# Two layers of a hybrid-heads and mixture-of-experts backbone: differential maps joined ahead of the turn, token lists in two stages, broadcast vectors issued later

## The reference

```python
def layer(x, xc, l):                      # 256 latent and 256 context tokens
    h = rmsnorm(x, norm1_g) * (1 + mod[1]) + mod[0]          # mod = silu(c) @ w_ada + b_ada
    y_a = window_attention(4 heads, with sinks)
    # differential attention, 4 heads of two maps each
    p = softmax(q0 @ k0.T) - lam * softmax(q1 @ k1.T);  y_b = rmsnorm(p @ v) * (1 - lam_init)
    y_c = latent_attention(4 heads);  y_d = gated_delta_net(4 heads, both directions)
    x = x + mod[2] * (concat(y_a, y_b, y_c, y_d) @ w_out)
    h = rmsnorm(x, norm2_g) * (1 + mod[4]) + mod[3]
    idx, w = top 6 of 64 experts for each token              # 4 of 8 groups first
    f = sum over idx of w * (silu(h @ w_gate[e]) * (h @ w_up[e])) @ w_down[e]
    x = x + mod[5] * (f + shared(h))                         # context alike in layer 0; layer 1 is latent only
```

## Time and profile before

| | |
|---|---|
| time, median of 3 executions | 2381.39 us (2380.7 to 2386.14) |
| time of the profiled execution | 2381.21 us |
| span of the profiled execution | 2379.4 us |
| PE busy | 2027.9 us, 85% |
| DVE busy | 705.3 us, 30% |
| ACT busy | 482.3 us, 20% |
| POOL busy | 261.7 us, 11% |
| moved by DMA | 558.55 MB, mean 235 GB/s |
| PE clock granted, mean share | 0.921 |

### The profile page before, as it was taken

The page is one execution under the profiler, slowest core; times in us unless marked ns, Lnnn a source line. Parts: engine busy times, 40 slices in busy tenths (PEclk is TensorE's granted clock), DMA queues, the critical chain, the costliest instruction groups (busy, mean ns, idle before and its releaser), DMA issues.

```text
span 2379.4 us, 33780 instructions
## 1 busy us (share of the span) xinstructions
PE 2027.9 (85%) x13844; PEld 1157.5 (49%) x13844; DVE 705.3 (30%) x1540; ACT 482.3 (20%) x1106; POOL 261.7 (11%) x312
## 2 busy tenths in 40 slices
PE   4999899979789999999993598899878888888982
PEld 2455578974534444444441356689753333333331
DVE  1121266651551111111113531666261111111114
ACT  1111265430201111111110211544211111111111
POOL 3000001210101111111110000022010111111110
PEclk9999999989789999999996699999888999999996
DMA  9576400001089999999987210100139999999963
GB/s 318 204 265 235 152 12 2 4 7 53 36 326 386 421 407 400 389 375 372 386 341 288 93 35 27 45 2 4 59 155 385 395 390 418 402 404 406 393 267 128
DMA packets 136120, 558.55 MB, mean 235 GB/s; under 512 B 27424, under 2 KB 60925, under 8 KB 85917
## 3 DMA queue, kind: packets, MB, share of 16 engines
q1 hardware_dynamic: 109757, 494.74, 52.0%
q0 software_dynamic: 24192, 38.54, 4.7%
q10 hardware_dynamic: 2016, 23.07, 2.3%
HBM read 556.26 MB, written 46.14 MB: 253 GB/s over the span
## 4 chain that ended last, share of the span: by engine, by line
PE 62%; DMA 23%; DVE 8%; ACT 2%; SPq 2%; issue 2%; POOL 0%; POOLq 0%; DVEq 0%; ACTq 0%
PE bank L760 55%; DMA arena<-in_moe_w_up 14%; DMA ring<-in_moe_w_up 7%; PE bank L763 6%; DVE arena L1268 2%; DVE arena L1265 1%; DMA arena<-y_rows 1%; DMA ring<-in_w_ada 1%; SPq L567 1%; ACT h_t L1909 1%; ACT arena L1909 1%; SPq L496 1%; DVE x_t L1268 1%; DVE arena L1291 1%; DVE arena L1809 1%
## 5 line engine op out<-in xcount | busy, mean ns | idle before, releaser
L760 PE MATMUL bank<-ring,arena 128*64 128x512 f32 (+4 forms) x2688 | 722.7, 523 | 70.1 <-DMA ring<-in_moe_w_up 47.1
L760 PE MATMUL bank<-arena 64*64 64x64 f32 (+6 forms) x5836 | 711.5, 323 | 44.9 <-DMA arena<-in_moe_w_up 21.0
L760 PEld LDWEIGHTS bank<-arena 64*64 64x64 f32 (+4 forms) x5836 | 367.8, 148 | 237.5 <-issue 222.6
L760 PEld LDWEIGHTS bank<-ring,arena 128*64 128x64 f32 (+3 forms) x2688 | 270.9, 152 | 367.1 <-issue 354.2
L763 PE MATMUL bank<-cst,arena 128*128 128x128 f32 (+2 forms) x1462 | 228.8, 296 | 124.6 <-DVE arena L1268 100.2
L1906 ACT ACTIVATE arena<-bank 128x256 f32<-128x256 f32 (+5 forms) x472 | 212.0, 459 | 587.7 <-PE bank L760 379.8
L763 PEld LDWEIGHTS bank<-cst,arena 128*128 128x128 f32 (+2 forms) x1462 | 190.1, 175 | 269.7 <-issue 131.5
L1265 DVE TENSOR_TENSOR arena<-arena,bank 128x256 f32<-128x256 f32 (+2 forms) x112 | 47.6, 425 | 740.5 <-ACT arena L1909 720.2
L760 PE MATMUL bank<-ring,h_t 128*128 128x384 f32 (+5 forms) x800 | 211.9, 427 | 17.4 <-ACT h_t L1909 17.4
L2308 POOL DMA_INDIRECT y_rows<-h_t,arena x80 | 80.4, 1005 | 933.7 <-DVE h_t L1844 933.7
L1909 ACT ACTIVATE arena<-bank 128x256 f32<-128x256 f32 (+1 forms) x86 | 33.4, 388 | 734.6 <-PE bank L760 734.6
(11 more groups left out here) (169 smaller groups left out, 1159.0 us busy)
## 6 DMA issues: line engine op xcount, KB each, us to landing
ring<-in_moe_w_gate SPq DMA_DIRECT2D x78, 1024.0 KB
ring<-in_moe_w_up SPq DMA_DIRECT2D x78, 1024.0 KB
ring<-in_moe_w_down SPq DMA_DIRECT2D x78, 1024.0 KB, 18.1
arena<-in_moe_w_gate SPq DMA_DIRECT2D x50, 1024.0 KB
arena<-in_moe_w_up SPq DMA_DIRECT2D x50, 1024.0 KB
arena<-in_moe_w_down SPq DMA_DIRECT2D x50, 1024.0 KB, 18.0
ring<-in_w_ada SPq DMA_DIRECT2D x52, 576.0 KB, 5.2
arena<-y_rows ACTq DMA_DIRECT2D x6, 3072.0 KB, 12.8
```

Of the source, the lines that this page charges most:

```text
L760: return pe.matmul(o, a, b, start=first, stop=last)
```

## The change

It has three parts.

1. **Differential maps** (`turned`, `turn_no`). When both exponentials of a differential head are there, DVE takes the reciprocals of their two sums, multiplies the second with the negative `lam` and the first map's sum, and adds the second map, so weighted, to the first. Only this one map is turned, copied and multiplied with the values. Turning comes one step later (two behind the scores) and the value product three behind, for all maps. `PX` has eight buffers in place of four; the added four lie in a slot of the ring. The scaling at the tile's end covers half the width.
2. **Token lists in two stages.** DVE makes 8 of the 16 rounds, which is enough for the pairs; three pairs lead the order of units. The other 8 rounds stand behind the copies of gathered rows of units 0 and 1, four each, and the whole units' lists are ordered on PE behind `up` of unit 1. The shared expert's products and sums are placed differently among them, and `down_bank` changes.
3. **Start.** POOL zeroes the padding, waits for PE's step `mod.turn 2` (the last before the projections) and then issues the 35 small transfers.

```diff
-    units, i = [(r,) for r in range(FIXED)], 0
-    for j, pair in enumerate(pairs):
-        upto = len(whole) * (j + 1) // n
+    units, i = [(r,) for r in range(FIXED)] + pairs[:RING], 0
+    for j, pair in enumerate(pairs[RING:]):
+        upto = len(whole) * (j + 1) // (n - RING)
...
-            return 2 + m % 6
+            return (4, 5, 2, 3, 6, 7, 1, 4)[m]
...
+        def turned(step):
+            return (2 * step, 2 * step + 1) if step % 8 < 4 else (2 * step,)
+        def turn_no(u):
+            return 12 * (u // 16) + (u % 16 if u % 16 < 8 else 4 + u % 16 // 2)
...
-                    for u in (2 * step - 2, 2 * step - 1):
+                    for u in turned(step - 2):
                         if 0 <= u < 2 * pairs:
-                            wait('ACT', 'att.exp', l, u)
+                            if u % 16 < 8:
+                                wait('ACT', 'att.exp', l, u)
+                            else:
+                                wait('DVE', 'att.less', l, u)
...
-                    for u in (2 * step - 4, 2 * step - 3):
+                    for u in turned(step - 3):
...
-                wait('DVE', 'rt.list', l, CAP // 8 - 1)
+                wait('DVE', 'rt.list', l, HALF // 8 - 1)
...
-                mm(bank[1][:, 0:full], LST[:, 0:CAP], PERM[:, 0:full])
...
+                    if u == 1:
+                        wait('DVE', 'rt.list', l, CAP // 8 - 1)
+                        mm(bank[7][:, 0:full], LST[:, 0:CAP], PERM[:, 0:full]).then_inc(*done('PE', 'rt.rest', l))
...
+                    u = 2 * step - 2
+                    if 0 <= u < 2 * pairs and u % 16 >= 8:
+                        wait('ACT', 'att.exp', l, u + 1)
+                        dve.reciprocal(RINV[:, i, m:m + 2], SUMS[:, i, m:m + 2]).then_inc(*done('DVE', 'att.rinv', l, i, m))
+                        wait('DVE', 'att.rinv', l, i, m)
+                        stt(RINV[:, i, m + 1:m + 2], RINV[:, i, m + 1:m + 2], lamt[:, 4:5], SUMS[:, i, m:m + 1]).then_inc(*done('DVE', 'att.share', l, u))
+                        wait('DVE', 'att.share', l, u)
+                        stt(PX[u % 8][:, 0:n], PX[(u + 1) % 8][:, 0:n], RINV[:, i, m + 1:m + 2], PX[u % 8][:, 0:n], ALU.mult, ALU.add
+                            ).then_inc(*done('DVE', 'att.less', l, u))
...
-                for r in range(CAP // 8):
-                    if r in (2, 7):
-                        shared_act((2, 7).index(r))
+                for r in range(HALF // 8):
+                    list_round(r)
+                    if r == 4:
+                        shared_act(1)
+                    if r == 6:
+                        shared_add(0)
...
+                    if isinstance(e, int) and e < 2:
+                        for n in range(4):
+                            list_round(HALF // 8 + 4 * e + n)
...
+            pool.memset(GP, 0.0).then_inc(*done('Pool', 'pad.zero', 0))
+            wait('PE', 'mod.turn', 0, 2)
             load_vectors(0)
             load_rows(pool, 1)
             load_vectors(1)
...
+                        if u == 0:
+                            wait('DVE', 'rt.tok2', l)
                         gather_rows(u + RING)
```

More of the change, by code:

```diff
@@ L266, in build @@
         CV, _ = area(at, 6, T)
-        CQT0, _ = area(at, 512)
-        PX = [PX3[:, q] for q in range(3)] + [area(at + 512, 512)[0]]
+        PX = [PX3[:, q] for q in range(3)] + [area(at + 512, 512)[0]] + [ring[:, 2 * SLOT + 2048 + 512 * q:2 * SLOT + 2560 + 512 * q] for q in range(4)]
         CQT, at = area(at, 2, T, parts=96)
@@ L950, in _ @@
                 pairs = 8 * tiles(l)
-                for step in range(pairs + 2):
+                for step in range(pairs + 3):
                     for u in (2 * step, 2 * step + 1):
@@ L1193, in _ @@
                 pe.wait_ge(m_sem(l, 'xg_loaded0'), 16)
+                wait('DVE', 'sh.x', l, 6, 0)
                 for c in range(KD):
@@ L1444, in _ @@
                 pairs = 8 * tiles(l)
-                for step in range(pairs + 3):
+                for step in range(pairs + 4):
                     for u in (2 * step, 2 * step + 1):
@@ L1707, in _, with shared_act, shared_add @@
                     dve.tensor_copy(HR[:, i, 0:512], bank[2][:]).then_inc(*done('DVE', 'rt.rows', l, i, 0))
+                def shared_act(f):
+                    wait('ACT', 'sh.silu', l, f)
+                    wait('PE', 'sh.up', l, f, 1)
+                    tt(SH2[:, f, 0:n_tok], SH1[:, f, 0:n_tok], bank[5 + 2 * f][:, 0:n_tok]).then_inc(*done('DVE', 'sh.act', l, f))
+                def shared_add(m):
+                    wait('PE', 'sh.down', l, m)
+                    for g in reversed(streams):
+                        q = slice(SEQ * g, SEQ * g + SEQ)
+                        stt(xT[:, m, q], bank[down_bank(m)][:, q], md[:, 40 + m, g:g + 1], xT[:, m, q], ALU.mult, ALU.add
+                            ).then_inc(*done('DVE', 'sh.x', l, m, g))
                 lg, ch = LG[:, 0:nt], CH[:, 0:nt]
@@ L1834, in rows_half @@
                     dve.tensor_copy(xgT[:, r, 0:512], bank[0][:]).then_inc(m_sem(l, 'xgT_dve'), 1)
+                    if isinstance(e, int) and e < 2:
+                        for n in range(4):
+                            list_round(HALF // 8 + 4 * e + n)
+                    if isinstance(e, int) and e == 2:
+                        wait('PE', 'rt.rest', l)
+                        codes_of(slice(0, full), bank[7][:, 0:full], 'rt.code2', 'rt.tok2')
                 def inner(e, r):
@@ L1852, in _ @@
                 with dve.If(dve.value_load(flags[0:1, l:l + 1], min_val=0, max_val=NE * CODES) > 0):
+                    wait('DVE', 'rt.drop', l, CAP // 8 - 1)
                     for r in range((n_tok - CAP) // 8):
@@ L2013, in _ @@
                 wait('Pool', 'kf.rope', l)
-                for step in range(pairs + 1):
-                    u = 2 * step - 2
-                    if u >= 0:
-                        n = P * len(key_tiles(u // 16))
-                        wait('PE', 'att.pt', l, u)
-                        if u >= 4:
-                            wait('PE', 'att.pv', l, u - 4)
-                        copy_out(PXT[:, u % 4, 0:n], bank[4 + u % 2][:, 0:n]).then_inc(*done('ACT', 'att.pt', l, u))
+                for step in range(pairs + 2):
+                    for u in turned(step - 2):
+                        if 0 <= u < 2 * pairs and turn_no(u) % 2 == 0:
+                            n, t = P * len(key_tiles(u // 16)), turn_no(u)
+                            wait('PE', 'att.pt', l, t)
+                            if t >= 4:
+                                wait('PE', 'att.pv', l, t - 4)
+                            copy_out(PXT[:, t % 4, 0:n], bank[4 + t % 2][:, 0:n]).then_inc(*done('ACT', 'att.pt', l, t))
                     for u in (2 * step, 2 * step + 1):
```

118 lines of the change are left out of this document (54 added, 64 removed).

## The result

The changed kernel takes 2368.18 us (median of 8 executions, 2357.93 to 2375.74), the kernel before 2382.72 (8 executions, 2380.7 to 2386.14).

What follows compares the result with a forecast made beforehand. Bounds: a transfer at the start, PE in attention, DVE's list in layer 0's routing, DMA and PE near balance in routed experts. Gains 10 + 14 + 9 + 3 = 36 from 2381.2 gave 2345 us; range 2331 to 2364.

Steps and rivals of the forecast that it cites:

- Start: Before the projections: without POOL's 35 transfers the awaited `w_ada` chunk lands sooner, net gain 10 us, lower bound 3.
- The first rival: Early projections: POOL's moved broadcasts collide with half chunks, giving back up to 8 of 10 us, 2353; chance 0.11.
- room: Early projections: DMA share was only 0.46 in a stretch, so most of POOL's moved queue fits; about 0.5 us given back.
- The starving of POOL's issues: Beside the projections: DVE's work slows POOL's issues; above 5.3 us each the kernel is slower by over 7.2 us; chance 0.03.
- Attention: Differential attention in both layers: fewer turns and value products gain 14 us, bounds 3 and 27.5.
- First tiles carry other DVE work: First attention tiles: DVE's extra work, including a reduction of 2.27 us, costs 1 us in each layer.
- The step itself: Attention's 512-key differential step: DVE's work sums to 2.70 us and sets it, against 3.81 before, gain 1.11.
- The second rival: Attention: joining takes 0.96 us and holds each turn, step above 3.1 us, gain only 5, 2354; chance 0.12.
- Routing and experts: Routing and routed experts: earlier lists and loads gain 9 us in layer 0 (3 to 14), 3 in layer 1 (0 to 4).
- The third rival: Routed experts: pairs in front only change which engine waits when, gain 0 in both layers, 2357; chance 0.13.
- The other eight rounds: Layer 0 routed experts: they cost DVE 2 x 6 us behind copies of units 0 and 1, hidden by `up`.
- no unit waited for its rows: Routed experts: a whole unit waiting for POOL's gathered rows would break the prediction; rows wanted past 717 us, lists there by about 714.

Runs made afterwards that it cites:

- experiment 7: Start and token lists changed together, attention code as before, against the kernel before: 2360.89 us, ratio 0.9882.
- experiment 4: Full change with DVE's 2.28 us reduction moved behind the fourth join, against the kernel before: 2353.53 us, ratio 0.9866.
- experiment 1: Kernel before with only the start changed (POOL's 35 transfers issued after PE's last turn ahead of the projections): 2371.41 us, ratio 0.9942.
- 5: Full change with six idle PE products ahead of the wait for the first tile's last join, both layers: 2358.79 us, ratio 0.9887 to the kernel before.
- 6: Full change with the late reduction, plus three and one idle PE products before attention's last two joins: 2352.48 us, ratio 0.9854 to the kernel before.
- 11: Full change with the late reduction and idle PE products in three attention waits, against the kernel before: 2345.59 us, ratio 0.9856.
- 9: Kernel before with only the attention part changed and the reduction moved behind the fourth join: 2371.93 us, ratio 0.9956.
- 3: Kernel before with only the attention part changed: 2387.7 us, ratio 1.0009.
- experiments 1 to 4: Start alone, lists alone, attention alone, and full change with late reduction, each beside the kernel before: 2371.41, 2374.03, 2387.7 and 2353.53 us.
- 10: Kernel before with only attention changed, late reduction, and idle PE products in three waits: 2369.99 us, ratio 0.9945.
- 12: Full change, late reduction, idle PE products in three waits, POOL's 35 transfers after the eleventh half chunk: 2357.0 us, ratio 0.9894 to the kernel before.

## Why the prediction was wrong

**Start: right, mis-sized.** Forecast 10 (3 to 11.1), measured alone 13.8 (9.3 to 18.4). The chunk came 14.7 us sooner, more than the 11.1 us of engine time that POOL's queue showed. That term was priced by busy share, and the bytes say more: SP's queue moved 6.06 MB in the first 30 us before and 11.21 in the changed kernel, and the 5.15 MB between them are 12.5 us at the 4.13 MB that it moves in the next 10 us. The last 2 us are open. The first rival, the collision, is real in some executions: PE waited for half chunks early in the projections for 3.7, 2.8 and 2.3 us in the traces of the full change, of experiment 7 and of experiment 4, and not at all in those of 1, 5, 6 and 11. It costs 2 to 5 us when it happens: at the end of the projections the three are 8.1 to 9.8 us ahead of before, the four 12.0 to 13.1. The "room" that I had read from one stretch of 3 us (a share of 0.46) wasn't there: the window below has 1.08. The starving of POOL's issues did not come. The full change's timeline has one of them, and the view by windows shows DVE busy all through that stretch (4.00 of 4.00 us):

```profile
51.55 0.61 POOL L2236 DMA_DIRECT2D bc<-in_gdn_a_log_f  x1
```

```profile
50.00:54.00 4.00, 4.00 (x6) 1.56 (x5) 4.00 (x11) 4.00 (x12) 4.00 (x9) 0.50 1.08 367
```

0.61 us, for 0.54 with DVE idle, and all 35 were issued in 18.6 us. The 3.1 us that the Trainium skill gives for a small transfer of POOL under a DVE copy ("SBUF — State Buffer", section "SBUF: two separate sides") are not seen on this trace's issues; but DVE made products of 256 columns there and no copies, so no run here tests the skill's own case.

**Attention: wrong.** Forecast 14 us less, measured 2 us more alone and about 12 more in the full change. The step that failed is "First tiles carry other DVE work (a reduction of 2.27) in these steps, for which I take off 1 us in each layer." I had set its cost as average load of DVE. It is an order: the reduction stands in DVE's list between the third join and the fourth, with the tile's results and the next tile's masked maxima behind it, and since the change PE needs the join. PE waits 3.06 us there, in both layers and in both kernels with this order (four of four). And I had no term at all for what follows such a wait: the granted clock falls (0.60 over 12 us), for 4.5 us more a layer. Moving one reduction gives back 15.5 us in the full change (experiment 4) and 12.6 alone (9 against 3); keeping PE busy during the wait, without shortening it, gives back 10.5 (5). With the reduction moved, most of the term stands where it is alone: 6.6 and 6.1 us in the two layers (table) for 7.8 and 6.2 worked out. In the full change it is 3.2 and 3.8, less by slow stretches such as those named under the table. The end of the stage gives some back too, since the 32 turns then take 5.4 us or more in both layers, for 5.35 and 3.69 before.

By the stage the full change loses 0.9 and 2.1 us, and 1.2 and 2.7 in the 32 turns behind it (6.50 and 6.38 us): 7 us of the 12; the other 5 are within the interval of 6. The trace of the part alone has the same 7 us, where its ratio gives 2 (from 2 less to 6 more), so one trace weighs it too high.

The step itself was mis-sized as well. I had worked out 2.70 us by adding up DVE's work. It is 3.16 us in the changed kernel. DVE waits 0.97 us for PE ahead of its maxima in it and PE 0.60 us for the join, so DVE's load alone doesn't set it. The second rival's sign, a step of 3.1 or more, so came, but not by its cause, as the join takes 0.67 to 0.75 and not 0.96, and it had foreseen a gain of 5 where there was none.

**Routing and experts: right.** Layer 0: first `up` 8.1 us sooner in its stage for 8, the load of the fourth slot 11 for 11.4. The routed stage gave back 1.3 us of it (first to last `up` 557.1 before, 558.4 after), so that 6.8 are left where I had taken 9. Layer 1: 2.0 us to the first `up` and 1.3 in the stage, 3.2 for 3. Together 10.0 in the trace and 10.5 (6.4 to 14.8) measured alone, for 12. The third rival (nothing stays) is refuted. The other eight rounds were hidden, and no unit waited for its rows at POOL.

**The sum.** 13.8 + 10.5 - 2 = 22 by the parts alone, 16.4 measured together. The rest is within the intervals of these measurements. I can't say more of it, because the executions themselves differ: eight of the full change lie 18 us apart, and eight of before 5.4, but seventeen of before, beside experiments 1 to 4, lie 14 apart. So it isn't shown that the change itself adds spread. The mean granted clock goes with it in the full change: 0.922 to 0.924 in the three fastest, 0.912 to 0.918 in the other five. Two places show how. The 32 turns at attention's end, always close behind a wait of 0.52 us for DVE, took between 3.7 and 6.5 us with the change's attention; with that of before (a wait of 0.84) 5.35 in layer 0 and 3.69 in layer 1, and the other way round in experiment 1. And in layer 0's third tile the same eight records, behind a wait of 1.14 to 1.18 us for a join, took 1.48 us in seven traces and 2.71 to 2.77 in three. So whether the clock falls behind a short wait differs between executions of the same instructions. That this makes up the spread fits the traces, but how it divides over the stages was not measured.

## What to carry to other kernels

When a result of an engine becomes a thing that PE waits for, read that engine's list in order between two such results, above all in the one step that has extra work: the average load doesn't tell. A wait of PE of some 3 us in a dense stage should be priced at its length plus the slow stretch behind it; here that was 3.1 and 4.5 us a layer. The cheap remedy was to move work that nobody waits for behind the join.

## What had not been expected of the hardware

- PE's clock: behind 3.06 us of waiting the twelve records took 5.3 us in place of 2.8, four times of four, at a granted clock of 0.60 where it was read. Behind waits of 0.6 to 0.9 us in the middle of the same stage PE kept its pace, behind 1.14 to 1.18 us in seven traces of ten, and at the stage's end, with waits of 0.2 to 1.7 us one after another, the turns were slow in all twelve places without idle products. Six useless products in the wait, longer than the wait itself (5.42 us), made the kernel faster.
- 35 small transfers of 0.74 MB in all, with 11.1 us of engine time, kept 5.15 MB of SP's queue from moving in 30 us and delayed a chunk of 3 MB by 14.7 us.
- A float32 product with 512 columns stands as two records, 0.43 us each, and takes 0.86 to 0.90 us of PE.
